# A gated convolution inside a two-block model kernel: the gated input made one chunk further ahead, its gate kept in a PSUM bank, seven taps in place of eight on TensorE

## The reference

```python
def conformer_conv(h, w_pw1, b_pw1, w_dw, b_dw, ln_g, ln_b, w_pw2, b_pw2):
    u = h @ w_pw1 + b_pw1
    a, gate = jnp.split(u, 2, axis=-1)
    u = a * jax.nn.sigmoid(gate)
    u = lax.conv_general_dilated(
        u, w_dw[:, None, :].astype(u.dtype), window_strides=(1,),
        padding=((CONV_WIDTH - 1, 0),),
        dimension_numbers=("NWC", "WIO", "NWC"),
        feature_group_count=D_MODEL) + b_dw
    u = jax.nn.silu(layer_norm(u, ln_g, ln_b))
    return u @ w_pw2 + b_pw2
```

## Time and profile before

| what | value |
|---|---|
| median of three runs | 3296.01 us |
| fastest and slowest of them | 3279.82 us, 3302.17 us |
| the profiled execution, whole | 3287.4 us |
| its span | 3285.5 us |
| TensorE busy | 3129.9 us, 95% |
| VectorE, ScalarE, GpSimd busy | 47%, 39%, 36% |
| mean granted TensorE clock | 0.974 of full speed |

### The profile page before, as it was taken

How to read it: one execution, slowest core, us unless ns; L and a number is a source line. 1 busy time by engine, 2 the same in 40 slices (tenths; PEclk the granted TensorE clock), 3 DMA queues, 4 the chain that set the end, 5 groups by cost and what they waited for, 6 DMA issues and landing times.

```text
span 3285.5 us, 40113 instructions
## 1 busy us (share of the span) xinstructions
PE 3129.9 (95%) x13790; PEld 2408.3 (73%) x13790; DVE 1550.0 (47%) x2245; ACT 1269.6 (39%) x1974; POOL 1178.6 (36%) x495
## 2 busy tenths in 40 slices
PE   7999999998998899999998998999989999899998
PEld 5655888886675578888855777888867787788886
DVE  6445555327625744553268633332247763333322
ACT  3234444323334534443322433443233343344432
POOL 3300444443343034444432532444432254144443
PEclk9988999999999899999999999999999999999999
DMA  3200323332220022323311321332322132133332
GB/s 134 83 17 8 96 90 95 97 101 77 83 90 14 1 69 92 95 91 101 98 52 52 115 85 47 94 93 92 103 82 64 59 110 87 42 91 94 96 96 89
DMA packets 73290, 260.51 MB, mean 79 GB/s; under 512 B 8528, under 2 KB 8792, under 8 KB 72928
## 3 DMA queue, kind: packets, MB, share of 16 engines
q1 hardware_dynamic: 68400, 249.07, 24.7%
q10 hardware_dynamic: 4784, 10.05, 0.9%
HBM read 256.97 MB, written 2.12 MB: 79 GB/s over the span
## 4 chain that ended last, share of the span: by engine, by line
PE 43%; issue 36%; POOL 14%; DVE 5%; ACT 1%; POOLq 0%; ACTq 0%; DMA 0%; DVEq 0%
POOL w_lo L503 14%; PE bank L563 11%; PE bank L564 11%; PE bank L565 11%; PE bank L954 2%; DVE bank L1630 2%; PE bank L1081 1%; PE bank L1084 1%; PE bank L639 0%; PE bank L902 0%; PE bank L1098 0%; PE bank L904 0%; PE bank L903 0%; DVE c_u L1616 0%; PE bank L675 0%
## 5 line engine op out<-in xcount | busy, mean ns | idle before, releaser
L503 POOL TENSOR_TENSOR w_lo<-w_raw,w_hi 128x1024 fp32r<-128x1024 f32 x475 | 1145.9, 2414 | 1975.0 <-ACT w_hi L1840 1975.0
L563 PE MATMUL bank<-xh,w_hi 128*128 128x512 f32 x2008 | 811.1, 404 | 37.8 <-DVE xl L1153 15.1
L564 PE MATMUL bank<-xl,w_hi 128*128 128x512 f32 x2008 | 800.5, 399 | 0.0
L565 PE MATMUL bank<-xh,w_lo 128*128 128x512 f32 x2008 | 799.9, 398 | 0.0
L1840 ACT ACTIVATE w_hi<-w_raw 128x1024 fp32r<-128x1024 f32 x475 | 500.9, 1056 | 661.1 <-DMA w_raw<-w_glu_out 156.2
L563 PEld LDWEIGHTS bank<-xh,w_hi 128*128 128x128 f32 x2008 | 381.1, 190 | 145.3 <-issue 24.7
L564 PEld LDWEIGHTS bank<-xl,w_hi 128*128 128x128 f32 x2008 | 381.2, 190 | 95.0 <-issue 4.3
L565 PEld LDWEIGHTS bank<-xh,w_lo 128*128 128x128 f32 x2008 | 381.0, 190 | 93.1
L1186 DVE TENSOR_TENSOR xt<-bank,xt 128x512 f32 x72 | 49.8, 692 | 502.1 <-PE bank L565 502.1
L565 PE MATMUL bank<-hh,w_lo 128*128 128x512 f32 x704 | 279.1, 396 | 0.0
L563 PE MATMUL bank<-hh,w_hi 128*128 128x512 f32 x704 | 279.1, 396 | 0.0
(11 more groups left out here) (309 smaller groups left out, 4410.7 us busy)
## 6 DMA issues: line engine op xcount, KB each, us to landing
w_raw<-w_ffn_in SPq DMA_DIRECT2D x88, 512.0 KB, 3.5
w_raw<-w_glu_in SPq DMA_DIRECT2D x88, 512.0 KB, 3.5
w_raw<-w_ffn_out SPq DMA_DIRECT2D x48, 512.0 KB, 3.5
w_raw<-w_glu_out SPq DMA_DIRECT2D x48, 512.0 KB, 3.5
w_raw<-w_ssm_in SPq DMA_DIRECT2D x41, 512.0 KB, 3.5
w_raw<-w_pw SPq DMA_DIRECT2D x24, 512.0 KB, 3.5
w_raw<-w_diff_in SPq DMA_DIRECT2D x24, 512.0 KB, 3.5
w_raw<-w_attn_in SPq DMA_DIRECT2D x18, 512.0 KB, 3.5
```

Of the source, the lines that this page charges most:

```text
L503: pool.tensor_tensor(w_lo[:, slot, :], w_raw[:, slot, :], w_hi[:, slot, :].bitcast(F32), ALU.subtract).then_inc(w_split, 1)
L563: pe.matmul(b, wh, hi[:, k, 0:n], start=(k == 0), stop=False)
L564: pe.matmul(b, wh, lo[:, k, 0:n], start=False, stop=False)
L565: mm = pe.matmul(b, wl, hi[:, k, 0:n], start=False, stop=last)
```

## The change

Four things change together, all in the convolution.

1. `CPE` is 7: TensorE does seven taps of a chunk, VectorE 24 (twelve of chunk p and twelve of chunk p - 1 in a round).
2. The gate stays in its PSUM bank: it is scaled, put through the sigmoid and read by `entered` there. The tiles `c_g` are gone, and the bank is given back by `entered` in place of `gated`.
3. `entered` runs one chunk further ahead: round p of VectorE makes chunk p + 2, near its end, and chunks 1 and 2 are made in round 0. There are four buffers of `c_u` in place of three.
4. TensorE does `project(2p + 4)` and `project(2p + 5)` behind `conv(p)` and the mean. `conv(1)` therefore has three projections ahead of it, where it had two. ScalarE's list is moved to match, with one `next_slab` more ahead of `m_hi`.

```diff
-        CPE = 8
+        CPE = 7
-        c_u = sb("c_u", [P, 3, CONVW - 1 + S])
+        c_u = sb("c_u", [P, 4, CONVW - 1 + S])
-        c_g = sb("c_g", [P, 2, S])
@@ TensorE: conv(p)
-                    pe.wait_ge(c_new, p + 1)
+                    pe.wait_ge(bank_free, BANKS + st.chunk0 + 2 * p + 2)
@@ TensorE: order
-                project(1)
-                for p in range(KD):
-                    if p < KD - 1:
-                        project(2 * p + 2)
-                    else:
-                        feed(KD)
+                for c in range(1, 3):
+                    project(c)
+                conv(0)
+                for c in range(3, 6):
+                    project(c)
+                for p in range(1, KD):
                     conv(p)
                     if p >= 3:
                         mean(p - 3)
-                    if p < KD - 1:
-                        project(2 * p + 3)
+                    if p < KD - 2:
+                        project(2 * p + 4)
+                        project(2 * p + 5)
+                    elif p == KD - 2:
+                        feed(KD)
@@ VectorE: gated(p), entered(p)
-                    if p >= 2:
-                        dve.wait_ge(c_new, p - 1)
                     dve.wait_ge(w_used, SLOTS + st.slab0 + 2 * p + 2)
-                    dve.tensor_tensor(c_g[:, p % 2, :], bank[(b0 + 1) % BANKS][:], rstd[:], ALU.mult).then_inc(bank_free, 1)
+                    dve.tensor_tensor(g[:], g[:], rstd[:], ALU.mult).then_inc(c_gate, 1)
...
-                    dve.scalar_tensor_tensor(c_u[:, p % 3, CONVW - 1:], c_a[:, p % 2, :], col("pw1_b", 2 * p),
-                                             c_g[:, p % 2, :], ALU.add, ALU.mult).then_inc(c_new, 1)
+                    dve.scalar_tensor_tensor(c_u[:, p % 4, CONVW - 1:], c_a[:, p % 2, :], col("pw1_b", 2 * p),
+                                             bank[(st.chunk0 + 2 * p + 1) % BANKS][:], ALU.add, ALU.mult).then_inc(bank_free, 1)
@@ VectorE: rounds
-                        if p < KD - 1 and n == (5 if p else 7):
-                            gated(p + 1)
-                        if p < KD - 1 and n == (7 if p else 9):
-                            entered(p + 1)
+                        if p == 0 and n == 2:
+                            gated(1)
+                        if p == 0 and n == 4:
+                            entered(1)
+                        if p < KD - 2 and n == 8:
+                            gated(p + 2)
+                        if p < KD - 2 and n == 9:
+                            entered(p + 2)
```

More of the change, by code:

```diff
@@ L426, in build @@
         o_raw, o_sq, o_sum, o_root, o_new = (sem(n) for n in ("o_raw", "o_sq", "o_sum", "o_root", "o_new"))
-        c_sig, c_new, c_dia, c_pe, c_step, c_done, c_out = (
-            sem(n) for n in ("c_sig", "c_new", "c_dia", "c_pe", "c_step", "c_done", "c_out"))
+        c_gate, c_sig, c_dia, c_pe, c_step, c_done, c_out = (
+            sem(n) for n in ("c_gate", "c_sig", "c_dia", "c_pe", "c_step", "c_done", "c_out"))
         c_msum, c_mrow, c_cent, c_csq, c_vsum, c_rec, c_norm, c_silu = (
@@ L953, in conv @@
                     for n in range(CPE):
-                        mm = pe.matmul(conv_bank(p)[:], c_diag[:, p % 2, n, :], c_u[:, p % 3, n:n + S],
+                        mm = pe.matmul(conv_bank(p)[:], c_diag[:, p % 2, n, :], c_u[:, p % 4, n:n + S],
                                        start=(n == 0), stop=(n == CPE - 1))
@@ L1596, in conf @@
                 norm_recip()
-                for q in range(3):
+                for q in range(4):
                     step(dve.memset(c_u[:, q, 0:CONVW - 1], 0.0))
                 def gated(p):
-                    b0 = st.chunk0 + 2 * p
-                    if p >= 2:
-                        dve.wait_ge(c_new, p - 1)
+                    a, g = bank[(st.chunk0 + 2 * p) % BANKS], bank[(st.chunk0 + 2 * p + 1) % BANKS]
                     dve.wait_ge(w_used, SLOTS + st.slab0 + 2 * p + 1)
-                    dve.tensor_tensor(c_a[:, p % 2, :], bank[b0 % BANKS][:], rstd[:], ALU.mult).then_inc(bank_free, 1)
+                    dve.tensor_tensor(c_a[:, p % 2, :], a[:], rstd[:], ALU.mult).then_inc(bank_free, 1)
                     dve.wait_ge(w_used, SLOTS + st.slab0 + 2 * p + 2)
-                    dve.tensor_tensor(c_g[:, p % 2, :], bank[(b0 + 1) % BANKS][:], rstd[:], ALU.mult).then_inc(bank_free, 1)
+                    dve.tensor_tensor(g[:], g[:], rstd[:], ALU.mult).then_inc(c_gate, 1)
                 def entered(p):
                     dve.wait_ge(c_sig, p + 1)
-                    if p >= 3:
-                        dve.wait_ge(c_done, p - 2)
-                        dve.wait_ge(c_pe, p - 2)
-                    dve.scalar_tensor_tensor(c_u[:, p % 3, CONVW - 1:], c_a[:, p % 2, :], col("pw1_b", 2 * p),
-                                             c_g[:, p % 2, :], ALU.add, ALU.mult).then_inc(c_new, 1)
+                    dve.wait_ge(bank_free, BANKS + st.chunk0 + 2 * p + 1)
+                    if p >= 4:
+                        dve.wait_ge(c_done, p - 3)
+                        dve.wait_ge(c_pe, p - 3)
+                    dve.scalar_tensor_tensor(c_u[:, p % 4, CONVW - 1:], c_a[:, p % 2, :], col("pw1_b", 2 * p),
+                                             bank[(st.chunk0 + 2 * p + 1) % BANKS][:], ALU.add, ALU.mult).then_inc(bank_free, 1)
                 taken = [0]
@@ L1625, in tap @@
                         dve.wait_ge(c_pe, p + 1)
-                        dve.wait_ge(c_new, p + 1)
+                        dve.wait_ge(bank_free, BANKS + st.chunk0 + 2 * p + 2)
                     else:
@@ L1629, in tap @@
                     k = CPE + n
-                    ins = dve.scalar_tensor_tensor(conv_bank(p)[:], c_u[:, p % 3, k:k + S], col("dw_w", CONVW * p + k),
+                    ins = dve.scalar_tensor_tensor(conv_bank(p)[:], c_u[:, p % 4, k:k + S], col("dw_w", CONVW * p + k),
                                                    conv_bank(p)[:], ALU.mult, ALU.add)
@@ L2144, in gate @@
                 def gate(p):
-                    act.wait_ge(bank_free, BANKS + st.chunk0 + 2 * p + 2)
-                    act.activation(c_g[:, p % 2, :], c_g[:, p % 2, :], ACT.Sigmoid, bias=col("pw1_b", 2 * p + 1))\
-                        .then_inc(c_sig, 1)
+                    act.wait_ge(c_gate, p + 1)
+                    b = bank[(st.chunk0 + 2 * p + 1) % BANKS]
+                    act.activation(b[:], b[:], ACT.Sigmoid, bias=col("pw1_b", 2 * p + 1)).then_inc(c_sig, 1)
                 def convolved(p):
@@ L2160, in conf @@
                 next_slab()
+                next_slab()
                 act.wait_ge(m_landed, 16)
@@ L2163, in conf @@
                 diag(1)
+                gate(1)
+                next_slab()
                 for p in range(KD - 1):
[L2165 to L2168, removed]
+                    if p < KD - 2:
+                        next_slab()
+                        gate(p + 2)
+                        next_slab()
                         diag(p + 2)
```

## The result

| | before | changed |
|---|---|---|
| median of 12 runs | 3291.91 us | 3269.74 us |
| fastest, slowest | 3279.82, 3302.17 | 3263.47, 3284.96 |
| span of the profiled execution | 3285.5 | 3267.6 |

The ratio of the two is 0.9941, with a 95% interval from 0.9923 to 0.9960: 13 to 25 us faster. The prediction was 3278.4 us, in a range of 3263 to 3293, with 17.6 us saved; the changed median is inside it, 8.7 us under the forecast, of which 4.1 are the median before, which twelve runs put at 3291.9 where three had put it at 3296.0. The profiled span fell by 17.9 us.

What follows compares the result with a forecast made beforehand. TensorE and VectorE waiting for each other in a loop over c_u bound the convolution. Out go 17.1 + 11.1 + 1.0 + 6.9 = 36.1 us, in come 18.5, net 17.6: 3296.0 - 17.6 = 3278.4 us, range 3263 to 3293.

Steps and rivals of the forecast that it cites:

- The loop opens: TensorE and VectorE stop waiting for each other over c_u: 17.1 us of waits and 11.1 of clock surplus go.
- a product in SBUF +6.5 us: VectorE's product at 2.4 us makes its round 19.4; five rounds lose 1.3 each, 6.5 us in all.
- The rule cited from the Trainium skill: VectorE instructions with two SBUF inputs contend with GpSimd instructions reading SBUF for a port pair; the PSUM gate frees the product.
- The other page's 65 ns more for a PSUM source: Extra VectorE latency of 62 cycles; about 1 us for eight products and eight gates, left out of the sum.
- Seven taps: TensorE loses eight taps of two records each, 6.9 us; VectorE gains eight, absorbed in the middle but not at the end.
- The start: Behind conv(0), m_hi late behind slab 6 makes TensorE wait 7.5 us, plus 2.5 us at the lower clock.
- The bounds for the surplus, 1.8 and 3.04: Limits in us on the 2.5 us clock loss behind the first wait, from surpluses behind short waits and the longest.
- The end: Ahead of mean(5), TensorE waits 6.0 us for VectorE's round 6 and a copy, plus 2.5 us of clock.
- the next bound: VectorE's last two rounds take 27.7 us against TensorE's 31.3 us of means and feed: not the bound by 2.8.
- The start was not clean: Rival: wait behind conv(0) stays near 1.9 us, 25.7 saved, 3270 us; chance 0.10 together with the everything-kind case.
- The taps kept their pitch: Rival: VectorE's taps slow from 0.66 to 0.79 us, making it the bound; net +2.2, 3298 us; chance 0.07.
- VectorE's turn: VectorE's work in one turn of the old loop, summed to 18.8 us, under the turn of 22.6 or 23.3.

Runs made afterwards that it cites:

- b_gate: Kernel before with only the gate kept in its PSUM bank; profiled stretch 176.9 us against 193.5, whole-kernel ratio 0.9952.
- a_ahead: Changed kernel with eight taps on TensorE, gate in SBUF and m_hi ahead of slab 6, leaving the larger distance alone; stretch 170.8 us (193.5 before the change).
- a_gate_sbuf: Changed kernel with the sigmoid's result written to SBUF and read there by the product; stretch 175.8 us against 175.4.
- the filler: Changed kernel with 38 useless matmuls on TensorE behind conv(0), in the first wait; stretch 172.4 us against 175.4.
- a_early: Changed kernel with m_hi and the diagonals of chunk 1 ahead of slab 6 again; stretch 168.7 us against 175.4.
- b_late: Kernel before with the upper part of slab 6 moved ahead of m_hi on ScalarE; stretch 197.8 us against 193.5.
- a_feed: Changed kernel with sixteen of the 48 feed steps moved ahead of mean(5); stretch 174.3 us against 175.4.
- a_cpe8: Changed kernel with eight taps on TensorE in place of seven; stretch 179.3 us against 175.4.

## Why the prediction was right

*The loop opens.* Predicted: the waits for `c_u`, 17.1 us, and their clock surplus, 11.1, go. Both went to nothing. Right as to what the change does. What the prediction did not see is that either of the two parts goes most of the way alone: the gate in its bank saves 16.6 (b_gate), the distance 22.7 (a_ahead). It priced the bank only inside the new order, and there it called a product in SBUF +6.5 us; it is +0.4 (a_gate_sbuf). That term's step, "VectorE would be the bound, and five rounds would lose 1.3 each", failed at its premise: the product is 0.75 us there as well, because the two engines hardly meet any more. The forecast itself took the value 0.75 and was not touched.

The rule cited from the Trainium skill, page "SBUF — State Buffer", section "🔬 SBUF: two separate sides", agrees with all of this: products with one SBUF input are 740 to 752 ns in b_gate, six of them beside GpSimd's subtraction; with two they are 2.1 to 2.6 us beside it and 747 to 769 ns with at most 0.2 us of overlap (a_gate_sbuf). The changed kernel's 735 to 749 ns do not test the rule, since there too the two engines hardly meet. The other page's 65 ns more for a PSUM source does not show: the medians are 740 (changed) and 748 ns (b_gate) from PSUM, 753 (a_gate_sbuf) and 744 (a_ahead) from SBUF.

*Seven taps.* Predicted 6.9 saved on TensorE, with a part given back at the end. Measured alone 7.1, in part by chance (above); inside the change 3.9, since at eight taps VectorE's late end and the first wait are shorter too.

*The start.* Predicted a wait of 7.5 and 2.5 of clock; measured 7.3 and, against the filler, 2.7. The mechanism, `m_hi` behind slab 6, is shown by a_early and b_late. The bounds for the surplus, 1.8 and 3.04, are too narrow: a_feed paid 1.5 behind a wait of 7.5 us.

*The end.* Predicted a wait of 6.0 and 2.5 of clock; measured 6.1, and from `mean(5)` to the end of the stretch 30.5 us where 31.3 was the sum, so 1.7 of clock if the other 28.8 are as before. That VectorE stands 2.8 us behind as the next bound was in the working, for the last copy alone. In a_feed not even these 2.8 came back, because `mean(6)` also waits for VectorE, for round 7, and sixteen feed steps stand behind it.

*The rivals.* The start was not clean. The taps kept their pitch: 18 in 11.95 us, 0.66 each, with the sigmoid in PSUM beside them. The size: 17.6 predicted, 18.1 in the stretch, 17.9 in the span, 19.4 by the ratio, 22.2 between the medians. That the stretch agrees within 0.5 us is in part luck: one surplus was 0.2 larger and the other 0.8 smaller than the sum had them, and the first alone came out 1.2 us apart in two executions of the same code. Two small slips in the working touch nothing: VectorE's turn adds up to 18.9 with the 8.00 that it names (18.8 with 7.91, from start to start), and 15.8 and 0.7 are 16.5.

## What to carry to other kernels

When two engines wait for each other in turn, look for the one instruction in the loop whose duration varies, and for what runs beside it; here one operand moved to PSUM gave 16.6 us, where a reordered schedule alone gave 22.7, and on top of that schedule the operand was worth 0.4. When work is moved ahead on one queue, list what stands behind it there and which other queue waits for that: one slab ahead of `m_hi` cost 6.7 us (a_early) and some 8.5 (a_cpe8 beside a_ahead) two engines away. A wait taken from one engine at the end of a stage is worth at most the distance to the engine that is late next, and in a_feed it was worth nothing, so move work between them with it.

## What the runs showed of the hardware that was not expected

A wait's cost in clock does not follow its length. Behind the 1.9 us wait of a_early the clock was at 0.60 for four microseconds. In the kernel before, the convolution that started at 1733.54 behind a wait of 2.32 us took 7.15, and its neighbour at 1755.02 behind one of 2.25 took 8.85. TensorE's timeline has their first records (the idle time is in the brackets):

```profile
1733.54 1.99 PE L954 MATMUL bank<-c_u,c_diag 128*128 128x512 f32 x4 [2.32 <-DVE c_u L1616]
...
1755.02 1.52 PE L954 MATMUL bank<-c_u,c_diag 128*128 128x512 f32 x2 [2.25 <-DVE c_u L1616]
```

And b_late shows the same loop paying 7.0 us, not 11.1, after a mere shift, and a_feed the same first wait paying 1.5, not 2.7. A surplus of 0.3 to 3 us for each wait of over 1.5 us is as close as this case lets one forecast it.

The spread of the runs is made ahead of the stretch. Its start lay between 1635.4 us (a_cpe8) and 1660.0 (a_both) in the thirteen profiled executions, although nothing there had been changed, and the granted clock up to 1600 us lay between 0.95 and 0.98; from the end of the stretch to the end of the span it was 1444.7 us before, 1445.7 changed, and 1444.3 to 1448.1 in all thirteen. For changes of some ten microseconds a stretch of the profile tells more than the whole time.
